# Six RMS-norm sums of squares: GpSimd adds the eight chunks, TensorE multiplies once

## What is computed

```python
def rmsnorm(x, g):
    xf = x.astype(jnp.float32)
    y = xf * lax.rsqrt(jnp.mean(xf * xf, axis=-1, keepdims=True) + EPS)
    return (y * g.astype(jnp.float32)).astype(x.dtype)

def _layer(x, l, pos, pool_hist, conv_buf, h0, mk, mv, P):
    hn = rmsnorm(x, P['norm_mix'][l])
    proj = hn @ P['w_in'][l]
    ...
    x = x + mixed @ P['w_out'][l]
    x = x + mem_attend(rmsnorm(x, P['norm_mem'][l]), mk, mv, P['w_mq'][l], P['w_mo'][l])
    hn = rmsnorm(x, P['norm_ffn'][l])
    ...
```

## Time and profile before

| | us |
|---|---|
| three runs | 1399.97, 1396.99, 1393.47 |
| their median | 1396.99 |
| span of the profiled execution | 1414.8 |
| PE / DVE / ACT / GpSimd busy in it | 1188.0 / 802.8 / 648.5 / 19.9 |

### The profile page before, as it was taken

The page is one execution under the profiler, slowest core; times in us unless marked ns, Lnnn a source line. Parts: engine busy times, 40 slices in busy tenths (PEclk is TensorE's granted clock), DMA queues, the critical chain, the costliest instruction groups (busy, mean ns, idle before and its releaser), DMA issues.

```text
span 1414.8 us, 20020 instructions
## 1 busy us (share of the span) xinstructions
PE 1188.0 (84%) x7722; PEld 1062.9 (75%) x7722; DVE 802.8 (57%) x1151; ACT 648.5 (46%) x876; POOL 19.9 (1%) x32
## 2 busy tenths in 40 slices
PE   6995009999999999898007999989999999999996
PEld 6995009756999999898007855879989989889895
DVE  5784006323755555587005422458878878878884
ACT  5672004213543344574003411337756757657663
POOL 0001000000000000001000000000000000000000
PEclk9998559999999999999557999869999999999998
DMA  7449934567555555448963566329969869878890
GB/s 297 152 149 44 12 25 169 205 207 261 164 180 189 179 181 179 144 151 84 15 23 111 180 223 238 144 70 339 363 212 359 316 225 361 306 269 315 305 341 32
DMA packets 64692, 273.00 MB, mean 193 GB/s; under 512 B 7552, under 2 KB 8000, under 8 KB 63968
## 3 DMA queue, kind: packets, MB, share of 16 engines
q1 hardware_dynamic: 62352, 264.33, 63.1%
q0 software_dynamic: 1824, 7.12, 3.1%
q10 hardware_dynamic: 432, 0.38, 0.1%
HBM read 265.83 MB, written 5.98 MB: 192 GB/s over the span
## 4 chain that ended last, share of the span: by engine, by line
PE 66%; DVE 12%; another core or an unknown queue 12%; ACT 6%; issue 3%; DMA 1%; DVEq 0%; ACTq 0%; SPq 0%
PE bank L580 9%; PE bank L582 8%; PE bank L581 8%; PE bank L577 8%; PE bank L578 8%; PE bank L579 8%; PE bank L715 4%; PE bank L759 3%; DVE wl L1362 3%; ACT wh L990 2%; PE bank L845 2%; PE bank L605 2%; DVE rstd L1357 1%; DVE sq L1373 1%
## 5 line engine op out<-in xcount | busy, mean ns | idle before, releaser
L577 PE MATMUL bank<-xh,wh 128*128 128x264 f32 x928 | 272.6, 294 | 183.5 <-DVE wl L1362 166.8
L1608 DVE TENSOR_TENSOR wl<-ring,wh 128x1408 fp32r<-128x1408 f32 x192 | 310.2, 1624 | 60.4 <-ACT wh L1229 60.1
L577 PEld LDWEIGHTS bank<-xh,wh 128*128 128x128 f32 x928 | 179.5, 193 | 190.1 <-issue 185.5
L1362 DVE TENSOR_TENSOR wl<-ring,wh 128x1024 fp32r<-128x1024 f32 x170 | 207.0, 1224 | 191.0 <-ACT wh L990 190.5
L1229 ACT ACTIVATE wh<-ring 128x1408 fp32r<-128x1408 f32 x189 | 261.1, 1381 | 85.9 <-PE bank L582 85.6
L990 ACT ACTIVATE wh<-ring 128x1024 fp32r<-128x1024 f32 x170 | 178.7, 1056 | 196.9 <-PE bank L579 143.2
L578 PE MATMUL bank<-xl,wh 128*128 128x264 f32 x928 | 268.2, 289 | 0.0
L579 PE MATMUL bank<-xh,wl 128*128 128x264 f32 x928 | 267.4, 288 | 0.0
L581 PE MATMUL bank<-wh,xl 128*128 128x352 f32 (+4 forms) x736 | 244.0, 332 | 0.0
L578 PEld LDWEIGHTS bank<-xl,wh 128*128 128x128 f32 x928 | 180.0, 194 | 0.0
L579 PEld LDWEIGHTS bank<-xh,wl 128*128 128x128 f32 x928 | 179.2, 193 | 0.0
(11 more groups left out here) (210 smaller groups left out, 1621.9 us busy)
## 6 DMA issues: line engine op xcount, KB each, us to landing
ring<-experts SPq DMA_DIRECT2D x192, 704.0 KB, 5.9
ring<-dense SPq DMA_DIRECT2D x234, 512.0 KB, 4.2
o_k<-kv POOLq DMA_DIRECT2D x2, 1024.0 KB, 4.7
o_v<-kv POOLq DMA_DIRECT2D x2, 1024.0 KB, 8.2
x<-xT SPq DMA_DIRECT2D x2, 528.0 KB, 5.0
o_y<-sq SPq DMA_DIRECT2D x4, 264.0 KB, 2.1
gatew<-gate_w POOLq DMA_DIRECT2D x2, 512.0 KB, 8.9
mem<-memT SPq DMA_DIRECT2D x1, 1024.0 KB, 13.2
```

The costliest lines, as they stand in the source:

```text
L577: mm(out, s_hi, m_hi, start=start, stop=False)
L1362: V.tensor_tensor(wl[:, k % NBUF, 0:UNIT], raw(u), wh[:, k % NBUF, 0:UNIT].bitcast(F32), ALU.subtract)\
L1608: V.tensor_tensor(wl[:, jj % NBUF, :], eraw(jj % ESLOTS), wh[:, jj % NBUF, :].bitcast(F32), ALU.subtract)\
```

## The change

The sum over chunks moves from PE to GpSimd. GpSimd waits for two squares, adds them into `rms[:, 1, :]` (called `summed`), and adds the other six one after the other, each after its own predecessor, seven adds of 128 x 264 a norm and 42 in all. PE waits for the seventh and multiplies the ones matrix by `summed` once (two passes instead of sixteen). The same six norms are changed; the memory's norm, the two norms of the mixing halves and the final norm are as before. Since GpSimd works through its queue in order, the adds are placed among its DMA starts, and the write of `o_k` moves from ahead of `o_v` to the end of the layer, behind the adds of the third norm.

```diff
+        summed = rms[:, 1, :]
...
+        chunks_summed = sem("chunk_squares_summed")
...
             def norm_sum(key, j):
                 n = tiles[key]
                 b = take_bank(n)
-                for m in range(KC):
-                    pe.wait_ge(sq_ready, KC * j + m + 1)
-                    i = mm(b[:, 0:T], ones[:, :], sq[:, m, :], start=(m == 0), stop=(m == KC - 1))
-                full(i, n)
+                pe.wait_ge(chunks_summed, (KC - 1) * (j + 1))
+                full(mm(b[:, 0:T], ones[:, :], summed, start=True, stop=True), n)
...
+            def sum_chunks(j):
+
+                for m in range(1, KC):
+                    pool.wait_ge(sq_ready, KC * j + m + 1)
+                    if m > 1:
+                        pool.wait_ge(chunks_summed, (KC - 1) * j + m - 1)
+                    G.tensor_tensor(summed, sq[:, 0, :] if m == 1 else summed, sq[:, m, :], ALU.add).then_inc(chunks_summed, 1)
+
             for l in range(DEPTH):
+                sum_chunks(3 * l)
...
-                for m in range(KC):
-                    wait_read(pool, tiles[key_tile(l, m)])
-                pool.dma_start(o_k[l], kT).then_inc(kv_written, 16)
...
+                sum_chunks(3 * l + 1)
+                sum_chunks(3 * l + 2)
+                for m in range(KC):
+                    wait_read(pool, tiles[key_tile(l, m)])
+                pool.dma_start(o_k[l], kT).then_inc(kv_written, 16)
```

## The result

The changed kernel takes **1406.81 us** (median of 20 runs) against 1397.04 us of the kernel before in the same comparison, a ratio of 1.0083 with a 95% interval of 1.0059 to 1.0108 (the two medians by themselves give 1.0070, the means of the twenty runs each 1407.2 and 1396.1). The change costs about 10 us. That is above the range of 1391 to 1406, on the side that had 13 chances in 100. The profiled execution of after has a span of 1399.2 us, shorter than the 1414.8 of before: the executions of one kernel spread over some 20 us, so two single ones can't be set against each other.

A forecast was written before the change was run, and what follows sets the result against it. PE's chain and the wait for small state writes bound the kernel; only the norms could win. Norms 1 to 5 at -3.9 us and norm 0 at +3.6 gave -0.3, from 1396.99 to 1396.7 us, range 1391 to 1406.

The forecast's parts named there:

- What bounds the kernel: PE's chain, plus DVE's 168.7 us wait before L1519, called untouched; at the six norms at most 7.0 us to win.
- The price of an add: GpSimd add of 128x264: 0.75 us plus 0.10 us hand-over, 0.85 us a step.
- Norms 1 and 4: Root at norm 1 at 229.68 instead of 230.64; 0.95 us gained at each of the two norms.
- Norms 2 and 3: ACT's table load is late next, so only 0.42 us gained at each of the two norms.
- Norm 5: Sixth add over before the last square comes; root at 903.37 instead of 904.54, 1.17 us gained.
- Norm 0: First norm gets slower by 3.6 us: 0.5 adds' pace, 1.1 contention with DVE's subtraction, 2.0 library request.
- The library request: New GpSimd request ahead of norm 0's first add, taken to end at 9.0 us and cost 2.0 us.
- Norms together: All six norms: -3.9 us at norms 1 to 5 and +3.6 us at norm 0, sum -0.3 us.
- What is moved: GpSimd's reordered transfers, some now behind the small writes, stay hidden: cost nothing, with an end of +1.5 us.
- The stall grows: Moved large transfers go between the small pieces, lengthening DVE's wait before L1519: +10.6 us, 1407; 8 in 100.
- The clock falls at the norms: PE's new idle time brings half-clock stretches of 3.4 us at two or three norms: +4 us, 1400.5; 7 in 100.

The follow-up runs named there:

- filler: Changed kernel with PE also multiplying six chunks of squares at each norm, results thrown away; ratio 1.0019 to the kernel before.
- e3: Kernel before, products still on PE, with only GpSimd's queue in the changed order (keys written at the layer's end); ratio 1.0056.
- e1: Kernel before, unchanged, timed and profiled once more as a control; ratio 1.0013.
- e5: Changed kernel with GpSimd waiting for all small state writes to land before it starts `o_v`, `gatew` and `poolw`; ratio 1.0037.
- e12: Changed kernel with the values' 1.05 MB written once more, to `o_y`, right behind `o_v`; ratio 1.0074.
- e4: Changed kernel with the adds, but `o_k`, `o_v` and the two loads in their old order behind the adds of norms 1 and 4; ratio 1.0057.
- the packed kernel: Six small states copied into one tile and written by one DMA; twelve-run means 1255.5 us without the change, 1252.2 us with it.

## Why the prediction was wrong, step by step

**What bounds the kernel**: right, and the stall that I named there as untouched is what the change touches.

**The price of an add**: 0.74 to 0.75 us, as taken; a step of the chain is 0.88 us (the adds of norm 0 start at 6.95, 7.84, 8.72 us) for 0.85.

**Norms 1 and 4**: 0.74 us and 0.73 us for 0.95. The product takes 0.68 us, not 0.61, and starts 0.14 us behind the last add, not 0.05. **Norms 2 and 3**: 0.20 and 0.41 for 0.42; at norm 2 the product ran at the lower clock (1.22 us) and came 0.23 us too late for ACT. **Norm 5**: 0.66 for 1.17, again with the product at the lower clock (1.01 us). Together 2.7 us for 3.9: the mechanism right, the size too large, because PE's idle time ahead of the product had no price in it.

**Norm 0**: the root moved from 13.60 to 15.20, +1.6 for +3.6. The adds' pace and the contention with DVE are as taken. The `wl` in question:

```profile
10.99 1.33 DVE L1362 TENSOR_TENSOR wl<-ring,wh 128x1024 fp32r<-128x1024 f32 x1 [4.85 <-ACT wh L990]
```

It took 1.33 for 1.23 us, and one add took 1.54 for 0.75: both share the price, 0.8 us on the adds and 0.1 on DVE. The library request cost nothing, not 2.0 us: the first add starts at 6.95, as soon as the second square is done. The Trainium skill (GPSIMD Engine Reference, Instruction dispatch) puts the first call into freshly loaded code at about 6 us; from 2.5 us on that gives 8.5, an estimate, and the trace doesn't agree. The add that was held starts at 11.38 us, when 0.94 us of DVE's operation lay ahead, and grew by 0.8 us. The Trainium skill (SBUF — State Buffer, on the shared port pair) excludes the two for a whole instruction; that fits the add, which stood for nearly all that was left of DVE's operation, and less so the `wl`, which started 0.24 us ahead of the end of an add and grew by 0.1.

**Norms together**: -2.7 + 1.6 = -1.1 us, against the forecast's -0.3. But the root of norm 0 was late in that one trace of before: in the eight traces with this sum on PE it starts at 12.17 to 13.60 us, mean 12.7, in the nine with adds and no filler at 15.11 to 15.27. So norm 0 costs 2.5 us rather than 1.6, and the norms together come to about nothing (-0.2). The forecast's -0.3 was right to a us, partly by luck: the gain at norms 1 to 5 and the loss at norm 0 were both taken some 1.1 us too large. It is not what decided.

**What is moved** is the step that failed. "I cost that at nothing because landings in this queue come in the order of the starts": e3 has the moved transfers and not one add, and its stall is 5 us longer (151.4 for 146.5; in the traces 149.7, and 144.6 in e1); e5 holds them back and the stall is 8 us shorter than after's (145.5 for 153.7; in the traces 142.1 for 150.1). I had read the earlier trace rows, three transfers that landed in the order of their starts with an empty queue ahead of them, as a rule for a queue with ten thousand small pieces in it. No row showed that case. The other term that the sum lacked is half-clock time, which stood among the rivals only. Histories and taps (the taps landed after 5.7 us) and `o_k` (DVE waited 2.44 us and had 1.10 left at L1624) came out hidden, as costed.

**The rivals.** *The stall grows* had 8 in 100 and was half of what happened: that the transfers go among the small pieces and lengthen the wait is right; the price was too high (10.6 for 6 to 7 us), and that the wait grows by the transfers' own time is refuted by e12. *The clock falls at the norms* had 7 in 100 and was the other part: stretches at half pace at norm 2 and ahead of norm 5's root, 84.7 against 74.2 us over all runs, some 4.5 us. Only part of that lies at the norms, where the rival looked for it: 3.4 us of half clock at norm 2 and 3.4 more at norm 5. The rest comes in the expert loop, more than 100 us behind norm 5, which nothing in the prediction had. I held against it that the new gaps were shorter than any in front of a drop; the traces have drops behind 1.9 and 2.1 us of waiting for the sum.

**The sum of after, as found**: stall +7.2 (153.7 - 146.5), half clock elsewhere +3.1 (0.43 x 7.2), norms -1.1; together +9.2, against 9.3 us between the means of the table (11.1 between those of the first comparison). With the norms at -0.2 it is +10.1; the terms aren't known to a us. Two causes that I took for exclusive, with 15 in 100 between them, came together. Either alone costs some 6 us (e3, e4), at the edge of what I called no change; that twice 6 is a little more than the 9 to 11 us of both together lies within the spread of the means.

**What stays open**: why large transfers lengthen the small writes by some 3 us a layer, and a further MB doesn't; what decides on half-clock time in the expert loop, and why norm 5's adds raise it with the stall in place and not without; and whether the adds gain 2 or 3 us in the packed kernel.

## What to carry to other kernels

When an edit puts instructions into an engine's queue, list the DMAs that it lets start earlier as carefully as those that it delays: a transfer that was late by accident may have been kept out of something's way. Here a stall of some 147 us (168.7 in the first profile) stood among the longest waits, twenty times the 7.0 us that the norms could give at most; six copies of 3.4 us in all and one transfer in place of six removed it (1397 to 1255 us). With it gone the change no longer costs time; whether it then saves the 1.5 to 2.5 us that the traces show outside the expert loop isn't settled. And where a kernel's own runs spread by more than the expected gain, split every timed run into its parts (here by the clock) before comparing.

## What the runs showed of the hardware

- Writes in pieces of 4 to 60 bytes: with some 10,000 pieces in a layer the last of six writes landed 84 to 98 us after its start (e1, after, before); the same data in 128 pieces of 2736 bytes landed in 4.5 us.
- Beside such pieces every transfer is slow: 1 MB started behind them in the same queue took 79 instead of 8 us, 512 KB of weights on SP's queue 79 instead of 3.4. The DMA engines were busy for 84 to 100% of the time at 20 to 24 GB/s.
- Large transfers behind them in the same queue go among them and lengthen the small ones by about 3 us a layer, in the first layer 1.8 MB as well as 2.8 MB.
- PE's granted clock fell from 2.4 to 1.2 GHz for 3.4 us at a norm where PE had waited 2.1 us for the sum, in nine of ten traces at one norm or more of 1, 2 and 4, and in none of ten where PE had products to do.
- A GpSimd add of 128x264 f32 takes 0.75 us, a step of dependent adds 0.88 us; 1.54 us beside a two-input DVE operation of 128x1024, which itself takes 1.33 instead of 1.23.
- GpSimd's first add after a library request at 2.5 us was not late at 6.95 us.
- The same stretch of matmuls, with the same 12.89 us of work ahead of it, ran at 2.4 GHz in one execution and at 1.2 in another; with one or two such stretches the 502 us from norm 5's root to the last root become 507 to 517.
